# Attention heads of short and long query tiles taken by turns, in a fused transformer kernel

## What is computed

```python
def forgetting_attention(q, k, v, log_f):            # layer 0 of the first stack, once: 8 heads of 64
    for blk in range(seq // Q_BLOCK):                # 4 query tiles of 128 rows
        lo, hi = blk * Q_BLOCK, (blk + 1) * Q_BLOCK
        s = q[:, lo:hi] @ k[:, :hi].T * scale + cum[lo:hi, None] - cum[None, :hi]
        p = softmax(where(causal, s, NEG_INF))
        outs.append(p @ v[:, :hi])

def nsa_mixer(...):                                  # second stack, both layers: 8 heads of 96, 2 kv groups
    for c in range(4):                               # query tiles; keys 0 .. 128*(c+1)
        o = g0 * o_cmp + g1 * o_slc + g2 * o_win     # three branches with gates
```

## Time and profile before

| | |
|---|---|
| median of 3 runs | 3818.21 us (3815.76 to 3835.15) |
| profiled execution | 3815.4 us, of which the span of the trace is 3813.6 us |
| PE busy | 3614.4 us (95%) |
| DVE, ACT busy | 1500.3 us (39%), 1240.3 us (33%) |
| mean granted clock | 0.962 |
| fox attention | 187 to 258 us of the span |
| cross-attentions | 417 to 457 us, 1206 to 1246 us |
| attentions of the second stack | 2172 to 2313 us (n0), 3242 to 3381 us (n1) |

### The profile page before, as it was taken

How to read it: one execution, slowest core, us unless ns; L and a number is a source line. 1 busy time by engine, 2 the same in 40 slices (tenths; PEclk the granted TensorE clock), 3 DMA queues, 4 the chain that set the end, 5 groups by cost and what they waited for, 6 DMA issues and landing times.

```text
span 3813.6 us, 40267 instructions
## 1 busy us (share of the span) xinstructions
PE 3614.4 (95%) x17809; PEld 3045.2 (80%) x17809; DVE 1500.3 (39%) x1654; ACT 1240.3 (33%) x1797; POOL 16.0 (0%) x33
## 2 busy tenths in 40 slices
PE   6998999998798999999999999999999999999998
PEld 6777788887587888888888877888888888778886
DVE  3534342336843323332235454233333344543233
ACT  2334232225743322232224243222322233432222
POOL 0000000000000000000000000000000000000000
PEclk9979999999899999999999799999999998899999
DMA  4303123221232232233222201322232223013321
GB/s 129 122 23 122 65 91 100 93 89 64 97 111 78 76 101 94 100 100 100 95 94 81 84 1 56 110 95 94 89 111 97 92 62 114 11 34 111 100 100 44
DMA packets 241982, 326.45 MB, mean 86 GB/s; under 512 B 19360, under 2 KB 210944, under 8 KB 241808
## 3 DMA queue, kind: packets, MB, share of 16 engines
q1 hardware_dynamic: 235984, 308.77, 24.7%
q0 software_dynamic: 4064, 14.71, 1.2%
q10 hardware_dynamic: 1760, 0.40, 0.1%
HBM read 321.74 MB, written 2.10 MB: 85 GB/s over the span
## 4 chain that ended last, share of the span: by engine, by line
PE 86%; DVE 8%; ACT 5%; issue 1%; ACTq 0%; DVEq 0%
PE P L447 26%; PE P L448 25%; PE P L449 25%; PE P L568 3%; PE P L547 3%; PE P L452 2%; DVE HT L1351 2%; ACT XN L908 1%; DVE BIG L1351 1%; ACT WR L901 1%; DVE X L1351 1%; ACT BIG L908 1%; DVE WR L1343 1%; DVE BIG L1360 1%; DVE BIG L1696 1%; DVE XN L1360 1%
## 5 line engine op out<-in xcount | busy, mean ns | idle before, releaser
L1343 DVE TENSOR_TENSOR WR<-STG,WR 128x2048 fp32r<-128x2048 f32 (+4 forms) x303 | 668.9, 2211 | 1456.3 <-ACT WR L901 1456.2
L447 PE MATMUL P<-HT,WR 128*128 128x512 f32 (+1 forms) x3080 | 1153.2, 374 | 77.0 <-DVE HT L1351 39.2
L448 PE MATMUL P<-HT,WR 128*128 128x512 f32 (+1 forms) x3080 | 1148.2, 373 | 0.0
L449 PE MATMUL P<-HT,WR 128*128 128x512 f32 (+1 forms) x3080 | 1147.4, 373 | 0.0
L901 ACT CAST WR<-STG 128x2048 fp32r<-128x2048 f32 (+4 forms) x303 | 556.4, 1843 | 1181.3 <-PE P L449 1181.2
L447 PEld LDWEIGHTS P<-HT,WR 128*128 128x128 f32 x3080 | 596.6, 194 | 180.6 <-DVE HT L1351 43.8
L449 PEld LDWEIGHTS P<-HT,WR 128*128 128x128 f32 x3080 | 596.1, 194 | 97.1
L448 PEld LDWEIGHTS P<-HT,WR 128*128 128x128 f32 x3080 | 596.8, 194 | 95.7
L447 PE MATMUL P<-WR,HT 128*128 128x512 f32 (+1 forms) x1344 | 523.8, 390 | 16.1 <-DVE HT L1351 16.1
L448 PE MATMUL P<-WR,HT 128*128 128x512 f32 (+1 forms) x1344 | 521.9, 388 | 0.0
L449 PE MATMUL P<-WR,HT 128*128 128x512 f32 (+1 forms) x1344 | 521.8, 388 | 0.0
(11 more groups left out here) (157 smaller groups left out, 2601.4 us busy)
## 6 DMA issues: line engine op xcount, KB each, us to landing
STG<-in_w_ffn_gu_dram SPq DMA_DIRECT2D x44, 1024.0 KB, 5.1
STG<-in_ffn_w_gate_dram SPq DMA_DIRECT2D x44, 1024.0 KB, 5.1
STG<-in_ffn_w_up_dram SPq DMA_DIRECT2D x44, 1024.0 KB, 5.1
STG<-in_ffn_w_down_dram SPq DMA_DIRECT2D x44, 1024.0 KB, 4.9
STG<-in_w_ffn_down_dram SPq DMA_DIRECT2D x22, 1024.0 KB, 4.8
STG<-in_w_xkv_dram SPq DMA_DIRECT2D x16, 1024.0 KB, 5.3
STG<-in_ab_w_in_dram SPq DMA_DIRECT2D x12, 1024.0 KB, 5.5
STG<-in_w_in_dram SPq DMA_DIRECT2D x12, 1024.0 KB, 5.2
```

Source lines behind the costliest of these rows:

```text
L447: pe.matmul(o, lh, rh, start=first, stop=False)
L448: pe.matmul(o, lh, rl, start=False, stop=False)
L449: return pe.matmul(o, ll, rh, start=False, stop=last)
L1343: v.tensor_tensor(WR[0:p, n % NWR, 1, cut], STG[0:p, n % NSTG, cut], WR[0:p, n % NWR, 0, cut].bitcast(F32), ALU.subtract).then_inc(ve.sem, ...
```

## The change

The order of the items changes: `two_lanes` starts with four heads of tile 0 and then alternates a head of the long tiles (3, then 2) with one of the short tiles (0, then 1), and ends with four heads of tile 2. Short tiles use one accumulator (lane 0), long ones the other (lane 1). The compressed branch's `out` of a tile now comes between its two plain branches, at step 15, 22, 47 or 54, and is added to what branch 0 has written; the other pieces move too. `out_proj` gets a point for each tile, so that its first tiles need not wait for the last one. The slots for the maximum are numbered by item, not by head.

```diff
-        N_OB = lambda br: O_BANK[1 - br]
+        lane = lambda t: 1 if t >= 2 else 0
+        turn_before = {3: None, 0: None, 2: 3, 1: 0}
+        cmp_before = {3: 0, 1: 3, 2: 1}
+
+        def two_lanes(parts):
+            short = [(t, part, h) for t in (0, 1) for part in parts for h in range(8)]
+            long = [(t, part, h) for t in (3, 2) for part in parts for h in range(8)]
+            order = short[:4]
+            for a, b in zip(long[:-4], short[4:]):
+                order += [a, b]
+            return order + long[-4:]
...
-                    for t in range(NT) for br in range(2) for h in range(8)]
+                    for t, br, h in two_lanes((0, 1))]
...
-            if i in (1, 3, 5):
-                return [({1: "norm", 3: "turn", 5: "out"}[i], 0)]
-            t, j = divmod(i, 16)
-            if j == 7 and t + 1 < NT:
-                return [("scores", t + 1)]
...
+            if late:
+                return {15: 0, 22: 3, 47: 1, 54: 2}.get(i)
+            return {1: ("norm", 0), 5: ("turn", 0), 17: ("scores", 3), 18: ("norm", 3), 20: ("turn", 3),
+                    40: ("scores", 1), 41: ("norm", 1), 43: ("turn", 1), 49: ("scores", 2), 50: ("norm", 2),
+                    52: ("turn", 2)}.get(i)
...
-                                g.wait_ge(*points(k))
+                                g.wait_ge(*points(k, t))
...
-                out_proj(s, 8, ht_operand, lambda k: ve.at(s, "olo", 3, 4))
+                out_proj(s, 8, ht_operand, lambda k, t: ve.at(s, "olo", t, k // 4 * 4))
...
-                    tt(ov4(N_ON[:, t % 2, :]), ov(0), wv(m8), ALU.mult, s, "co", t)
+                    tt(ov4(N_TMP), ov(O_BANK[lane(t)]), wv(m8), ALU.mult, s, "co", t)
+                    g.wait_ge(*ve.now())
+                    tt(on, on, N_TMP, ALU.add)
+                    g.wait_ge(*ve.now())
```

More of the change, by code:

```diff
@@ L1311, in hook @@
                 def hook(i):
[L1312 to L1316 removed]
+                    part, t = nsa_hook(i) or ("", 0)
+                    if part == "scores":
+                        scores(t)
+                    if part == "turn":
+                        cmp_turn(t)
                 scores(0)
```

138 lines of the change are left out of this document (69 added, 69 removed).

## The result

| | before | after |
|---|---|---|
| median, range (4 runs each) | 3816.99 us (3806.93 to 3835.15) | 3878.81 us (3875.31 to 3879.85) |
| ratio | | 1.0145, 95% interval 1.0107 to 1.0183 |
| profiled execution, span | 3815.4, 3813.6 | 3877.86, 3876.0 |
| PE busy; mean granted clock | 3614.4; 0.962 | 3647.3; 0.954 |
| fox (first score to `out_proj`, with the wait ahead) | 79.1 us | 104.1 us |

The change costs 62 us, where +22 was forecast, and 3878.8 lies above the forecast's range, which ended at 3867. The page of the changed kernel, busy times and granted clock in 40 slices (compare): PE's work is the same 17809 records, but they take 33 us longer, and that is clock: the trace's clock records have 360.1 us at half clock instead of 295.6.

A forecast was written before the change was run, and what follows sets the result against it. PE, busy 3614.4 us or 95% of the span, was taken to bound the kernel. The terms 28 + 6 - 13 + 3.4 + 2.5 - 4.5 gave +22 us on 3815.4, forecast as 3840, range 3800 to 3867.

The forecast's parts named there:

- part 3: Clock of n0 and n1: an earlier rise, -13 us, and one more half-clock stretch in each, +3.4 us.
- part 4: Fox: the clock returns near 230 us at output transposes, no gain or loss; remaining pairs wait, +2.5 us.
- Part 1: n0 and n1: long items' products wait for the copy behind the exponential, 14.0 us in each, +28 us.
- Part 2: n0 and n1: VectorE's work ahead of a maximum or of freeing an accumulator counts in full, +3 each, +6 us.
- A: The forecast itself, 3840 us, with fox's clock rising near 230 us; chance 0.36.
- rival B: In fox the clock stays at half to the end, +23.5 us, 3864 us; chance 0.25.
- rival D: Fox's clock comes back some 30 us sooner, at tile 3's wide scores, -15 us, 3825 us; chance 0.10.
- Part 5: The gaps of 1.40, 1.56 and 1.56 us ahead of out_proj in fox, x0 and x1 go, -4.5 us.
- E: PE hardly waits in n0 and n1, a pair taking less than about 3.2 us; 3788 us; chance 0.13.
- C: The waits of Part 1 in n0 and n1 are half as large, 3826 us; chance 0.13.

The follow-up runs named there:

- Copy first: The changed kernel with ScalarE's copy for item i-2 placed ahead of the exponential of item i; 3815.6 us, ratio 0.9984 to the kernel before.
- Compressed second: The kernel before, tile order, with the compressed output at item 10 of its tile and the next tile's compressed scores at item 13; 3843.6 us, ratio 1.0070.
- its early product: As Compressed second, but PE's compressed product at item 7 and scaled at once, only the addition waiting; 3804.2 us, ratio 0.9971 to the kernel before.
- the lanes in fox only: The kernel before with the two-lane order of items in fox alone; 3838.8 us, ratio 1.0027 to the kernel before.
- the waits by tile alone: The kernel before with out_proj's waits given for each tile and nothing else; 3792.1 us, ratio 0.9899 to the kernel before.
- T: The kernel before, tile order, with out_proj's waits by tile and ScalarE's copy ahead of its exponential; 3802.0 us, ratio 0.9949 to the kernel before.
- the pair with 16 extra matmuls: The kernel before and the changed kernel, each with an extra 128x512 matmul ahead of every second fox head's scores; 3812.5 and 3860.5 us.

## Why the prediction was wrong

The copy's wait, the forecast's main cost, came close to its price. Two steps failed: the clock of n0 and n1 (part 3) and the clock of fox (part 4).

**Part 1, right.** Forecast: the pair 4.04 us with a wait of 1.17. Measured: 4.15 and 1.01. "14.0 in each" stands against 11.3 us of products waiting for `ACT XN L1003` in n0, 16 times, and 1.6 us of such waits ahead of transposes. With the copy first they are all gone.

**Part 2, right in sum, wrong in what it says of the branch.** PE's idle time grew by 15.4 us in n0 (forecast 14.0 and 3). The waits at the first product of branch 1 came as priced (1.33 and 1.49 us at two of them, "1.4 to 1.5"). But I priced them as waits only. In tile order alone the compressed branch's new place, with four such waits, made n0 and n1 14.4 and 12.6 us longer.

**Part 3, the step that failed in n0 and n1.** The rise came even earlier than forecast: 13.7 us behind the fall instead of the 19 that 2187 would have made. What failed is the sentence "I take one more such stretch in each", of 3.5 us, which makes two in each behind the first rise. There were four in n0 (41.0 us) and five in n1 (37.5). The term was -13 + 3.4; with 102.4 us at half clock in the two instead of 70.1 it was +16. I priced each wait once, as idle time. I had also misread the one example: I wrote that the fall at 2277.5 came behind "a compressed output and a piece of waiting", but PE's last wait before it was 0.27 us long and ended at 2259.7. PE's timeline of the kernel before, there:

```profile
2274.61 2.02 PE L834 MATMUL P<-FX,BIG 31*128 31x96 f32 x16
2276.57 1.15 PE L547 MATMUL P<-BIG 96*128 96x512 f32 x2
2277.53 0.29 PE L550 MATMUL P<-MB 128*128 128x128 bf16 x1
```

So here the compressed output's narrow matmuls were followed by 3.4 us of half clock with no wait near them (those of tiles 1 and 2, at 2208.0 and 2238.2, were not); with a wait beside them it was 6.8 to 13.7 in n0 of the changed kernel, and the new order puts all four outputs beside waits. Compressed second and its early product show the same pair in tile order: with the 2 us waits behind the outputs 55 us of n0 are at half clock, without them 27. Copy first shows that the copy waits lengthen these falls but do not make them: without any, the four are there still, for 23.9 us instead of 41.0. How the two work together, no run separates further.

**Part 4, the step that failed in fox.** I took A, that the clock returns near 230; in the profile it stayed at half to the end, and the other three runs lie within 5 us of that one, which is rival B with its +23.5 (measured +25.0). B's 3864 was still 15 us short, mostly by the clock of n0 and n1. Place and time were right: the output transposes of tile 0 came at 227.06. Only the outcome was not. The copy-first kernel, whose PE order is the same, shows the other one. Its PE timeline and windows of fox:

```profile
227.46 1.06 PE L459 MATMUL P<-CST,BIG 128*128 128x128 f32 x4
228.31 1.06 PE L552 MATMUL P<-BIG 66*128 66x256 f32 x2
...
230.52 1.08 PE L552 MATMUL P<-BIG 66*128 66x512 f32 x2
```

```profile
185.30:229.70 44.40, 41.67 (x155) 31.27 (x156) 14.82 (x34) 14.07 (x43) 0.00 (x0) 0.50 0.08 24
229.70:258.00 28.30, 26.52 (x198) 22.03 (x198) 14.71 (x33) 14.12 (x40) 1.10 (x2) 1.00 0.06 23
```

And the changed kernel's timeline at the same place, where scores of 512 keys still take 2.02 us instead of 1.08:

```profile
227.06 1.06 PE L459 MATMUL P<-CST,BIG 128*128 128x128 f32 x4
227.91 1.06 PE L552 MATMUL P<-BIG 66*128 66x256 f32 x2
...
230.90 2.02 PE L552 MATMUL P<-BIG 66*128 66x512 f32 x2
```

In all nine profiles without float32 matmuls among the heads in which the clock rose in fox, it did so 0.8 to 2.6 us behind the start of a group of output transposes (228.0 in the earlier trace rows, 205.8, 205.8, 204.9, 227.5, 229.3, 223.8, 231.4, 228.1), never elsewhere. But not every group brings it: in the changed kernel, the lanes in fox only, the waits by tile alone and T all four passed without. So the place was right, and whether the clock rises there was chance as far as I could tell from the rows; I should have given B as much as A. That the transposes themselves bring it is not shown, as no run took them away and left the rest. The Trainium skill's rule, "TensorE: Matmul & The Clock Gate", Part 4, that transposes don't count as work the way other matmuls do, sits badly with these nine rises, but they do not refute it; rival D, which I worked out beside it, did not come either. With its clock apart fox costs +6.9 us (the pair with 16 extra matmuls), forecast 2.5 less 1.4.

**Part 5, right and short.** The gaps are gone (-3.7 us in the cross-attentions). The rest, -8.3, I had at nothing. Of it 4.5 are the stretch between x1 and n0, which every kernel with waits by tile shows, and 1.6 the stretch between x0 and x1; the other 2.2 are spread over stretches that also differ from profile to profile, the one ahead of fox most (177.5 to 181.2 us).

**The rivals.** E is out: the pair takes 4.15 us, far above its 3.2. C is out too: idle time grew by 15.4 us of the forecast 17 in n0. The sum on the forecast's own terms, with what they measured: 30.8 (idle) + 16 (clock of n0 and n1) + 2.6 (not assigned) + 25.0 (fox) - 3.7 - 8.3 = 62.4.

## What to carry to other kernels

Price a wait on TensorE that stands beside narrow matmuls twice: its own length, and the half clock that may follow it. Here four waits of 2 us in an attention cost 20 us, and removing 23 us of waits gave 38. Four waits of 1.0 us between wide products cost their own length only. When one engine's program holds a copy behind a function of a later item, look there before the order of the items; putting the copy first gained 38 us of n0 and n1 in one order and 7 to 13 in the other. And where a stretch's length takes distinct values from run to run, pin it (here by eight extra matmuls) before small things are compared, and do it to both sides.

## What the hardware showed that I had not expected

- Fox runs at half clock for 24, 44 or some 100 us in tile order, and for 44 or 100 in two lanes; kernels with the same program for PE differ in it. Full-width float32 work among the short heads ended that, for 6.8 us of added work; 30 fp32r matmuls of the same width right ahead of the attention did not.
- PE can be busy nearly all the time and stay at half clock: from 183.1 to 285.5 PE was busy for 98.45 of 102.40 us, at 0.50.
- A single wait of 2 us a few us behind the compressed output had 3.4 to 17.1 us at half clock beside it, eight times of eight in n0 and n1 of one kernel, while four waits of 1.0 us in a row between wide products had none. A compressed output with no wait near it was followed by 3.4 us at half clock (2277.5 in the kernel before).
- Removing the wait ahead of x1's `out_proj` and its kin shortened a stretch of pure weight products, hundreds of us long, by 4.5 us, by clock alone (PE idle 12.1 us in both), in all fifteen profiles that have the edit. How it reaches that far stays open.
